# An encoder's expert stage: branches in place on TensorE, full columns in the down matmuls, and three loads moved

## The chip, the cores and the metric
The kernel runs on the 8 cores of one Trainium2 chip. Each core works on one of the 8 sequences of the batch by itself, with no exchange between cores. The metric is the device time of the slowest core in microseconds. Five engines run side by side on each core: TensorE (PE in the profile, its weight loads PEld), VectorE (DVE), ScalarE (ACT), GpSimd (POOL) and SyncE (SP). Here POOL and SP issue nearly all transfers.

## The reference
Input is x (8, 2048, 1024) in float32. Two pre-norm residual layers follow: a token mixer (grouped attention, latent attention and a gated linear attention, merged by gates), then a feed-forward part. In the second layer that part is a mixture of experts, and it is what this case is about:

```
logits = einsum('btd,de->bte', h, w_router)
top_v, top_i = top_k(logits, 2);  top_w = softmax(top_v)
gate = sum over k of top_w * one_hot(top_i, 8)
for e in range(8):
    out += gate[..., e:e+1] * ((silu(h @ w_gate[e]) * (h @ w_up[e])) @ w_down[e])
```

Here h is the RMS-normed x (width 1024) and an expert is 3584 wide. Each token goes to 2 of 8 experts, so of the 2048 tokens of a core 512 go to an expert on average. A last RMSNorm with the gains g_final closes the model.

## The kernel before, in words
**A list of operations.** The program is written as a list: `S.op(engine, fn, reads, writes, ...)` records one operation, a Python function that emits its instructions (one, or many matmuls), with the keys that it reads and writes. `order()` then works out each engine's order from estimated costs, and `run()` emits each engine's stream, with semaphore waits that `waits_for` puts ahead of an operation (L382).

**The expert stage** (`moe`). The router writes for each token the slots that it takes in its two experts (indirect scatters from POOL into a table `mt` in DRAM, L1554). For each expert, `expert_tokens` reads the expert's part of the table (SP, L1576 and L1579), gathers the tokens' rows (five indirect loads from POOL, L1583), and transposes them on TensorE into `xgT` (L1594). `expert_block` then does two stages. In the first, 14 weight blocks `wgu` of 1 MB (three buffers) each give two chunks of 128 hidden columns; `swiglu_chunk` makes for each chunk two TensorE operations (gate, up) of 16 matmuls: 8 steps of the contraction, by two segments of tokens (L1364). ACT and DVE turn them into `aT` (L1374, L1375). In the second, the down stage, 2 halves of the output by 7 weight blocks `wdn` of 0.5 MB (five buffers) give 14 TensorE operations (L1654): `aT` is the stationary side, 128 tokens at a time, and each tile of tokens has a PSUM bank. The results are scaled on ACT and DVE and scattered to DRAM by POOL (L1673). The transposes of the next expert's tokens stand between the first down operations. The last expert also runs the sums (`combine`), and the final norm (`token_rms`, `token_scale`) comes behind it. All weight loads are on POOL's queue; `load_first` issues those of the first expert (3 `wgu`, 5 `wdn`) ahead of the router's end where their buffers are free.

**Levels.** How many tokens an expert gets is known only at run time. `LEVELS = ((512, 256), (560, 256), (608, 304))` gives three sizes with the length of the first segment: at level 0 an operation of the down stage has 4 chunks by 4 tiles of tokens, 16 matmuls; at level 1 there is a fifth tile of 48 tokens, at level 2 of 96, so 20 matmuls. The router leaves each expert's level in `C.level`. TensorE's operations of an expert have the attribute `sel` (expert, address of its level, operation that wrote it) and `alts`, one function for each level. Only TensorE branches. If an expert has more than 608 tokens, all engines enter an overflow section (`cond_section`, L441, L442); it doesn't happen with these inputs.

**Where the branch stands.** `stretches` cuts TensorE's order into groups. An operation without `sel` is a group by itself, but from the first operation of an expert to its last everything is one group, the next expert's transposes with it. `choose` emits a group: it loads the level into a register (L390), and then

```
with eng.If(v > 1):
    body(2)
with eng.Else():
    with eng.If(v > 0):
        body(1)
    with eng.Else():
        body(0)
```

so the code of an expert stands three times in a row, level 2 first. The profile gives the test of the outer `If` to L403, and to L406 both the inner test and the jump over the code of level 0 behind the code of level 1.

Of the kernel before, what the change touches and what calls it, by code (L numbers as in the profile page):

```python
# [6 lines left out]
F32 = mybir.dt.float32  # L7
BF16 = mybir.dt.bfloat16
# [5 lines left out]
D = 1024  # L14
# [4 lines left out]
NEXP = 8  # L19
DFFE = 3584  # L20
# [3 lines left out]
CAP = 608  # L24
CAPT = (CAP + 127) // 128
# [103 lines left out]
class Sched:  # L129
    def __init__(self, nc, es):  # L130
        self.nc = nc
        self.es = es
        self.ops = []
        self.last_writer = {}
        self.readers = {}
        self.dma_sems = {}
        self.dma_last = {}
        self.eng_ops = {e: [] for e in ENGS}
        self.tiles = {}
        self.top = (nc.sbuf_base + 63) // 64 * 64  # L140
        self.uid = 0

    def alloc(self, stack, name, shape, dt):
        off = self.top
# [240 lines left out]
    def choose(self, eng, group, wm):  # L385

        first = self.ops[group[0]]
        level_ap, level_op = first["sel"][1:]
        self.waits_for(eng, {level_op}, wm)
        v = eng.value_load(level_ap)  # L390
        after = {}

        def body(k):
            w = dict(wm)
            for idx in group:
                o = self.ops[idx]
                self.waits_for(eng, o["deps"], w)
                ins = (o["alts"][k] if o["alts"] else o["fn"])(eng)
                if o["needed"]:
                    key, sem, val = self.event(o)  # L400
                    ins.then_inc(sem, 1)
            after.update(w)
# [7 lines that stand above are left out]
        wm.update(after)  # L410

    def stretches(self, ename):

        order = self.eng_ops[ename]
        last = {}
        for n, idx in enumerate(order):
            if self.ops[idx]["sel"] is not None:
                last[self.ops[idx]["sel"][0]] = n
        n = 0
        assert sorted(last.values()) == [last[k] for k in sorted(last)]  # L420
        while n < len(order):
            sel = self.ops[order[n]]["sel"]
            if sel is None:
                yield [order[n]]
                n += 1
            else:
                yield order[n:last[sel[0]] + 1]
                n = last[sel[0]] + 1

    def run(self, ename, eng, final_waits=()):  # L430
        wm = {}
# [1174 lines left out]
def load_gu(C, S, n, s):  # L1606
    S.op("pool", lambda e: e.dma_start(out=C.wgu[s][:], in_=C.dr["wE"][n]), writes=[("wgu", s)], dma=f"wgu{s}")

def load_dn(C, S, n, s):
    S.op("pool", lambda e: e.dma_start(out=C.wdn[s][:], in_=C.dr["wEd"][n // 14, n // 7 % 2, n % 7]), writes=[("wdn", s)], dma=f"wdn{s}")  # L1610

def load_first(C, S):
    for n in range(3):
        load_gu(C, S, n, n)
    for n in range(5):
        load_dn(C, S, n, n)

def expert_block(C, S, ex, m, n, segs, hook=lambda name, i: None, sel=None):
    dr, TT = C.dr, C.TT
    NC = DFFE // 128  # L1620
# [3 lines left out]
    for g in range(NC // 2):  # L1624
        n_ = C.wi
        C.wi += 1
        s = n_ % 3
        if n_ >= C.ahead[0]:
            load_gu(C, S, ex * 14 + g, s)
        wv = C.wgu[s][:].rearrange("p (v c k m) -> p v c k m", v=2, c=2, k=8)  # L1630
        for c in range(2):
# [3 lines left out]
                         lambda a, b, ch=ch: C.aT[:, ch, a:b], [("aT", ch, i) for i in range(len(segs))], sel)  # L1635
        hook("p1", g)
    C.S = saved
    for half in range(2):
        bk = [(half * 5 + i) % 8 for i in range(nt)]
        for q in range(NC // 4):  # L1640
            n_ = C.wj
            C.wj += 1
            s = n_ % 5
            if n_ >= C.ahead[1]:
                load_dn(C, S, ex * 14 + half * 7 + q, s)
            wv = C.wdn[s][:].rearrange("p (c m) -> p c m", c=4)

            def fn(e, q=q, wv=wv, bk=bk, n=n, h=n):
                ins = None
                for c in range(4):  # L1650
                    for i in range((n + 127) // 128):
                        w = min(128, n - i * 128)
                        at = i * 128 if i * 128 < h else HALF + i * 128 - h
                        ins = e.matmul(C.ps[bk[i]][0:w, :], C.aT[:, 4 * q + c, at:at + w], wv[:, c, :], start=(q == 0 and c == 0), stop=(q == NC // 4 - 1 and c == 3))  # L1654
                return ins
            alts = [lambda e, fn=fn, m=m_, h=h if m_ < CAP else m_: fn(e, n=m, h=h) for m_, h in LEVELS] if sel else None
            down = S.op("pe", fn, reads=[("wdn", s)] + [("aT", 4 * q + c, i) for c in range(4) for i in range(len(segs))], writes=[("ps", b) for b in bk], alts=alts, sel=sel)
            hook("p2", half * 7 + q)
            if sel:
                C.behind = [down]  # L1660
        for i in range(nt):
            y_i = C.yi % 4
            C.yi += 1
            yst = C.yst[y_i]
            w = wd[i]
            col = i if w == 128 else CAPT - 1
            sc, rd = C.mtab[m][0:w, col, 2:3].bitcast(F32), [("ps", bk[i]), ("mtab" if w == 128 else "mtabr", m)]
            if i % 2:
                S.op("act", lambda e, yst=yst, b=bk[i], sc=sc, w=w: e.activation(out=yst[0:w, :], in_=C.ps[b][0:w, :], func=AF.Copy, scale=sc), reads=rd, writes=[("yst", y_i)])  # L1669
            else:  # L1670
                S.op("dve", lambda e, yst=yst, b=bk[i], sc=sc, w=w: e.tensor_scalar(out=yst[0:w, :], in0=C.ps[b][0:w, :], scalar1=sc, scalar2=None, op0=ALU.mult),  # L1671
                     reads=rd, writes=[("yst", y_i)])
            S.op("pool", lambda e, yst=yst, col=col, half=half, w=w: e.indirect_dma_start(  # L1673
                out=dr[f"yt{half}"], out_offset=bass.IndirectOffsetOnAxis(ap=C.mtab[m][0:w, col, 1:2], axis=0), in_=yst[0:w, :], in_offset=None),
                reads=[("yst", y_i), ("mtab" if w == 128 else "mtabr", m)], writes=[("yt", ex, i, half)], dma=f"yst{y_i}")

def moe(C):
    S, dr, sbt, TT = C.S, C.dr, C.sbt, C.TT
    ph = C.es.enter_context(ExitStack())
    one = S.arena(C.hbase + NT * D * 4)  # L1680
# [1 line left out]
    C.wgu = [one("wgu", [128, 4096], BF16) for _ in range(2)]  # L1682
    ntail = [(one.at[0] - base[0]) // 2048]
    assert one.at[0] == C.wbase - 8 * T * 2
    C.aT = one("aT", [128, DFFE // 128, CAP], BF16)
    base.append(one.at[0])
    C.xgT = one("xgT", [128, 8, CAPT * 128], BF16)
    C.sgf = [one("sgf", [128, 512], F32) for _ in range(2)]
# [9 lines left out]
    C.wdn += [one("wdn", [128, 2048], BF16) for _ in range(2)]  # L1698
    C.sq = [one("sq", [128, D], BF16) for _ in range(2)]
    ygt = [one("ygt", [128, 512], F32) for _ in range(4)]  # L1700
    C.load_gain(one, 4)
    C.wgu.append(S.arena(S.nc.sbuf_top - 8192)("wgu", [128, 4096], BF16))
    assert one.at[0] <= S.nc.sbuf_top - 8192
    C.wi = C.wj = C.yi = C.ffi = C.wm = 0
# [19 lines left out]
            tail.extend(over("ytl", [128, 512], F32) for _ in range(n))  # L1724
        gi[0] = 0

    load_first(C, S)
    sub = overflow(C)
    S.cond_section(C.flag[0:1, 0:1], "flag", sub)
    ts, m = expert_tokens(C, S, 0, 0, CAP, "tr", [0, 1, 2, 3])  # L1730
    for t in ts:
        t()
    segs = [(0, CAP // 2), (CAP // 2, CAP)]
    for ex in range(NEXP):
        nxt, nm = [], [0]

        def hook(name, i, ex=ex, nxt=nxt, nm=nm):
# [2 lines left out]
                nxt.extend(ts)  # L1740
            if name == "p2" and i < 5 and nxt:
                nxt.pop(0)()
            if ex == NEXP - 1 and name == "p1" and i >= 2:
                for half in range(2):
                    combine(i - 2, 0, half, ygt, "ygt")
# [53 lines left out]
```

How the kernel before makes its waits and increments, by code:

```python
    def waits_for(self, eng, dset, wm):  # L370
        need = {}
        for d in dset:
            key, sem, val = self.event(self.ops[d])
            if val > need.get(key, (None, 0))[1]:
                need[key] = (sem, val)
        for key, (sem, val) in need.items():
            if key[0] == "e":
                if any(k[0] == "e" and k[1] == key[1] and k[2] > key[2] for k in wm):
                    continue
            if wm.get(key, 0) >= val:
                continue
            eng.wait_ge(sem, val)
            wm[key] = val
# [9 lines left out]
        def body(k):  # L393
            w = dict(wm)
            for idx in group:
                o = self.ops[idx]
                self.waits_for(eng, o["deps"], w)
                ins = (o["alts"][k] if o["alts"] else o["fn"])(eng)
                if o["needed"]:
                    key, sem, val = self.event(o)
                    ins.then_inc(sem, 1)
            after.update(w)
# [27 lines left out]
    def run(self, ename, eng, final_waits=()):  # L430
# [16 lines left out]
            else:  # L447
                ins = o["fn"](eng)
            if o["dma"] is not None:
                ins.then_inc(self.dsem[o["dma"]], 16)
            elif o["needed"]:
                key, sem, val = self.event(o)
                ins.then_inc(sem, 1)
        self.wm = wm
        for (e2, name) in final_waits:
            if e2 == ename and name in self.dsem:
                eng.wait_ge(self.dsem[name], self.dma_sems[name]["total"])
```

## Time and profile before

| | |
|---|---|
| runs (3) | 4669.5 us median, 4656.28 to 5200.78 |
| the profiled execution | 4663.14 us |
| its span on the slowest core (3) | 4661.6 us |
| spans of the 8 cores | 4575.8 to 4661.6 us |
| granted TensorE clock | 0.965 to 0.970 of full speed |
| PE, DVE, ACT, POOL busy on core 3 | 90%, 41%, 42%, 19% |
| first expert's first matmul, last expert's last matmul | 3130.8 us, 4613.8 us |

A busy share is an average over stages, and the matmuls' ends are modelled, so what a change is worth is read from the chain of work that ended last and from the stretch that it touches. In that chain a line is a start, a length and what ran in it; "issue" is time in which the engine waited for nothing that the profile shows, and here it holds the branches. All times are from the start of the span.

### The profile page before, as it was taken

To read this page: it belongs to the slowest core of one execution; us is meant where nothing else is said; L and a number is where in the kernel's file an instruction comes from. 1 tells how busy PE (TensorE), PEld (TensorE's weight loads), DVE (VectorE), ACT (ScalarE), POOL (GpSimd) and SP (SyncE) were. 2 spreads that over 40 slices of the span, in tenths; PEclk is the share of its full clock that TensorE was granted. 3 is DMA by queue.
4 is the path that set the end of the run, shared out by engine and by line. 5 is a ranking of instruction groups with operands and counts; after the bars stand their busy time and mean duration, and the time that the engine had idled before them with its cause. 6 is when DMAs were issued, how large, how long until landed. Compare 5 with 4: busy or idle time off the path is not lost.

```text
span 4661.6 us, 73833 instructions; the slowest of 8 cores (4575.8 to 4661.6 us)
## 1 busy us (share of the span) xinstructions
PE 4180.5 (90%) x25337; PEld 2225.0 (48%) x25337; DVE 1926.7 (41%) x3537; ACT 1964.7 (42%) x2884; POOL 907.3 (19%) x959
## 2 busy tenths in 40 slices
PE   5888988899999999898988899959989999998895
PEld 3444433334444444444433344537638647465571
DVE  3767676752331223758585832442102112111133
ACT  5777687852331213777687742321101111011112
POOL 0111222233200000111222233331111211201101
PEclk9999999999999999999999999979999999999998
DMA  4000211032484331000301132538868977677876
GB/s 115 10 11 1 47 33 38 29 63 41 100 188 83 89 78 46 2 10 2 65 29 38 30 62 38 121 61 152 154 121 143 165 126 141 124 133 132 166 160 207
DMA packets 115186, 390.90 MB, mean 84 GB/s; under 512 B 19040, under 2 KB 30688, under 8 KB 95584
## 3 DMA queue, kind: packets, MB, share of 16 engines
q0 software_dynamic: 63856, 275.09, 33.9%
q1 hardware_dynamic: 50928, 110.52, 7.4%
q8 instruction: 245, 4.01, 0.4%
q14 instruction: 157, 1.29, 0.1%
HBM read 576.85 MB, written 49.61 MB: 134 GB/s over the span
## 4 chain that ended last, share of the span: by engine, by line
PE 74%; DVE 7%; issue 7%; DMA 5%; ACT 5%; POOL 1%; DVEq 0%; ACTq 0%; SPq 0%; POOLq 0%
PE ps L1364 22%; PE ps L712 20%; PE ps L1654 10%; PE ps L826 4%; PE ps L834 4%; PE ps L1423 3%; PE ps L835 3%; ACT PTb L831 2%; PE ps L827 2%; ACT PT L831 2%; DMA wgu<-wE 1%; PE ps L1117 1%; DMA ygt<-yt 1%; PE ps L1142 1%; DMA xr<-x 1%
## 5 line engine op out<-in xcount | busy, mean ns | idle before, releaser
L1364 PE MATMUL ps<-xgT,wgu 128*128 128x256 bf16 (+1 forms) x7168 | 854.4, 283 | 102.7 <-issue 78.0
L1364 PEld LDWEIGHTS ps<-xgT,wgu 128*128 128x128 bf16 x7168 | 710.7, 99 | 246.9 <-issue 109.1
L1374 ACT ACTIVATE sgf<-ps 128x304 f32<-128x304 f32 (+1 forms) x536 | 216.6, 451 | 1019.4 <-PE ps L1364 998.1
L1375 DVE TENSOR_TENSOR aT<-ps,sgf 128x304 bf16<-128x304 f32 (+1 forms) x536 | 248.5, 505 | 931.6 <-PE ps L1364 914.0
L831 ACT ACTIVATE PTb<-ps 128x1024 bf16<-128x1024 f32 x512 | 501.7, 1027 | 91.9 <-PE ps L827 78.4
L831 ACT ACTIVATE PT<-ps 128x1024 bf16<-128x1024 f32 x512 | 502.6, 1033 | 73.5 <-PE ps L827 55.3
L1654 PE MATMUL ps<-wdn,aT 128*128 128x512 bf16 (+1 forms) x2072 | 510.9, 383 | 11.9 <-DVE yst L1671 8.9
L712 PE MATMUL ps<-hT,wm 128*128 128x512 bf16 x1536 | 362.5, 380 | 0.0
L1654 PEld LDWEIGHTS ps<-wdn,aT 128*128 128x128 bf16 (+1 forms) x2072 | 179.6, 98 | 337.0 <-issue 194.1
L1364 PE MATMUL ps<-hT,wf 128*128 128x512 bf16 x1408 | 307.0, 381 | 6.7 <-DMA wf<-wF 5.4
L1302 ACT ACTIVATE sg<-ps,vec 128x512 bf16<-128x512 f32 x192 | 131.9, 689 | 345.3 <-PE ps L712 343.7
L712 PEld LDWEIGHTS ps<-hT,wm 128*128 128x128 bf16 x1536 | 150.5, 98 | 181.7 <-issue 2.2
L826 PE MATMUL ps<-qb,kh 128*128 128x512 bf16 x512 | 194.1, 379 | 39.6 <-ACT PTb L831 35.9
L834 PE MATMUL ps<-PT,Va 128*128 128x512 bf16 x512 | 199.3, 389 | 26.0 <-DVE num L850 13.5
L1364 PEld LDWEIGHTS ps<-hT,wf 128*128 128x128 bf16 x1408 | 137.9, 98 | 173.9 <-issue 10.4
L1669 ACT ACTIVATE yst<-ps,mtab 128x512 f32<-128x512 f32 x32 | 20.3, 686 | 475.5 <-PE ps L1654 475.5
L1220 DVE SCALAR_TENSOR_TENSOR Sbf<-Sst,dec,ps 128x128 bf16<-128x128 f32 x512 | 175.6, 343 | 91.2 <-PE ps L1204 36.9
L834 PE MATMUL ps<-PTb,Vb 128*128 128x512 bf16 x512 | 193.7, 378 | 7.3 <-DVE numb L850 4.3
L1671 DVE TENSOR_SCALAR yst<-ps,mtab 128x512 f32<-128x512 f32 (+1 forms) x48 | 34.4, 745 | 399.4 <-PE ps L1654 334.7
L835 PE MATMUL ps<-PT,Va 128*128 128x512 bf16 x512 | 197.3, 385 | 0.0
L827 PE MATMUL ps<-qb,kh 128*128 128x512 bf16 x512 | 194.4, 380 | 0.0
L835 PE MATMUL ps<-PTb,Vb 128*128 128x512 bf16 x512 | 193.8, 379 | 0.0
(239 smaller groups left out, 6241.6 us busy)
## 6 DMA issues: line engine op xcount, KB each, us to landing
wgu<-wE POOLq DMA_DIRECT2D x112, 1024.0 KB, 9.7
wdn<-wEd POOLq DMA_DIRECT2D x112, 512.0 KB, 6.9
xr<-x SPq DMA_DIRECT2D x51, 512.0 KB, 5.1
wf<-wF POOLq DMA_DIRECT2D x22, 1024.0 KB, 10.1
ropeA<-ropeA SPq DMA_DIRECT2D x40, 512.0 KB, 4.0
wm<-wM POOLq DMA_DIRECT2D x48, 384.0 KB, 4.5
x<-xr SPq DMA_DIRECT2D x32, 512.0 KB, 3.9
wCh<-wC POOLq DMA_DIRECT2D x8, 1024.0 KB, 8.4
```

The source lines that it names most:

```text
L712: ins = e.matmul(out, l_, r_, start=(i == 0), stop=(i == n - 1))
L826: e.matmul(ps[b][:], k_ap(2 * kp), q_ap(0), start=True, stop=True)
L827: return e.matmul(ps[b + 1][:], k_ap(2 * kp + 1), q_ap(1), start=True, stop=True)
L831: S.op("act", lambda e, b=b, p_i=p_i: e.activation(out=PT[p_i][:], in_=C.psall[:, b * 512:b * 512 + 1024], func=AF.Exp, scale=scale), read ...
L834: e.matmul(acc[:], v_ap(2 * kp), PT[p_i][:, 0:512], start=(kp == 0), stop=False)
L835: return e.matmul(acc[:], v_ap(2 * kp + 1), PT[p_i][:, 512:1024], start=False, stop=(kp == NT // 2 - 1))
L1220: S.op("dve", lambda e, ch=ch, cur=cur, nb_=nb_, dcol=dcol: e.scalar_tensor_tensor(out=Sbf[nb_][:], in0=Sst[cur][:], scalar=dec[:, dcol:dc ...
L1364: ins = e.matmul(pk[v * n + i][0][:, 0:b - a], w(v, c, k), rhs(k, a, b), start=(k == 0), stop=(k == 7))
L1374: S.op("act", lambda e, pg=pg, sg=sg, m=b - a: e.activation(out=sg[:, 0:m], in_=pg[0][:, 0:m], func=AF.Silu), reads=[pg[1]], writes=[("sgf ...
L1375: S.op("dve", lambda e, pu=pu, sg=sg, m=b - a, a=a, b=b: e.tensor_tensor(out=out(a, b), in0=pu[0][:, 0:m], in1=sg[:, 0:m], op=ALU.mult), r ...
L1423: ins = e.matmul(C.ps[b0 + half], aT[:, c, TT(tl)], wd[:, c, half * 512:(half + 1) * 512], start=(c == 0), stop=(c == NC - 1))
L1654: ins = e.matmul(C.ps[bk[i]][0:w, :], C.aT[:, 4 * q + c, at:at + w], wv[:, c, :], start=(q == 0 and c == 0), stop=(q == NC // 4 - 1 and c ...
```

## The change
Four things change. (1) TensorE's operations of an expert are cut into groups of at most four consecutive ones, and every group has its own three bodies and its own tests; the level is loaded into a register once for each expert. (2) The down matmuls always load 128 columns of `aT`: `aT` gets 128 more columns, set to zero once, and is read as one flat tensor, so that a tile of 48 or 96 tokens takes in columns of the next chunk; the operation then also depends on that chunk. (3) The final gains are loaded when the sixth expert's first block is done, no longer at the start of the expert stage. (4) The loads of the fourth and fifth down weight block of the first expert wait until its last gather has landed.

```
     def choose(self, eng, group, wm):
         first = self.ops[group[0]]
-        level_ap, level_op = first["sel"][1:]
-        self.waits_for(eng, {level_op}, wm)
-        v = eng.value_load(level_ap)
+        ex, level_ap, level_op = first["sel"]
+        if ex not in self.levels:
+            self.waits_for(eng, {level_op}, wm)
+            self.levels[ex] = eng.value_load(level_ap)
+        v = self.levels[ex]
...
     def stretches(self, ename):
-        order = self.eng_ops[ename]
-        last = {}
-        for n, idx in enumerate(order):
-            if self.ops[idx]["sel"] is not None:
-                last[self.ops[idx]["sel"][0]] = n
-        n = 0
-        assert sorted(last.values()) == [last[k] for k in sorted(last)]
-        while n < len(order):
-            sel = self.ops[order[n]]["sel"]
+        group = []
+        for idx in self.eng_ops[ename]:
+            sel = self.ops[idx]["sel"]
+            if group and (sel is None or len(group) == 4 or sel[0] != self.ops[group[0]]["sel"][0]):
+                yield group
+                group = []
             if sel is None:
-                yield [order[n]]
-                n += 1
+                yield [idx]
             else:
-                yield order[n:last[sel[0]] + 1]
-                n = last[sel[0]] + 1
+                group.append(idx)
+        if group:
+            yield group
...
-def load_dn(C, S, n, s):
+def load_dn(C, S, n, s, extra=()):
...
-def load_first(C, S):
+def load_first(C, S, late=None):
     for n in range(3):
         load_gu(C, S, n, n)
     for n in range(5):
-        load_dn(C, S, n, n)
+        if n < 3 or late is None:
+            load_dn(C, S, n, n)
...  expert_block, down stage
-                        w = min(128, n - i * 128)
                         at = i * 128 if i * 128 < h else HALF + i * 128 - h
-                        ins = e.matmul(C.ps[bk[i]][0:w, :], C.aT[:, 4 * q + c, at:at + w], wv[:, c, :], start=..., stop=...)
+                        at += (4 * q + c) * CAP
+                        ins = e.matmul(C.ps[bk[i]][:], C.aTf[:, at:at + 128], wv[:, c, :], start=..., stop=...)
...
-            down = S.op("pe", fn, reads=[("wdn", s)] + [...], ...)
+            down = S.op("pe", fn, reads=[("wdn", s), ("aT", 4 * q + 4, 0), ("aT", 4 * q + 4, 1)] + [...], ...)
...  moe
-    C.aT = one("aT", [128, DFFE // 128, CAP], BF16)
+    width = DFFE // 128 * CAP
+    C.aTf = one("aT", [128, width + 128], BF16)
+    C.aT = C.aTf[:, 0:width].rearrange("p (c t) -> p c t", c=DFFE // 128)
+    S.op("pool", lambda e: e.memset(C.aTf[:, width:width + 128], 0.0), writes=[("aT", DFFE // 128, 0)])
...
-    C.load_gain(one, 4)
+    C.gain = one("gain", [128, D], F32)
...
-    load_first(C, S)
+    load_first(C, S, True)
...
     ts, m = expert_tokens(C, S, 0, 0, CAP, "tr", [0, 1, 2, 3])
+    for n in (3, 4):
+        load_dn(C, S, n, n, [S.last_writer[("xs", CAPT - 1)]])
...  in hook
+            if ex == NEXP - 3 and name == "p1" and i == 0:
+                S.op("sp", lambda e: e.dma_start(out=C.gain[:], in_=dr["gains"][4]), writes=["gain"], dma="gain", extra=[S.last_writer[("aT", 0, 0)]])
```

## Rows read from the trace of the kernel before
**Rows 1.** The cores: span and mean granted TensorE clock.
```profile
core 3: 4661.6 us, clock 0.969
core 4: 4638.5 us, clock 0.968
...
core 7: 4589.6 us, clock 0.965
```
**Rows 2.** Chain that ended last, core 3, expert stage: start us, us, what.
```profile
3090.06 13.33 DMA mt<-meta,idx
...
3121.60 9.17 issue
3130.77 100.18 PE ps L1364 x896
...
3258.65 24.35 PE ps L1654 x112
...
3284.59 2.48 issue
...
3441.28 36.36 PE ps L1654 x140
...
3479.22 15.35 issue
...
3843.16 11.08 issue
```
**Rows 3.** The same view of core 1, a down stage at level 2.
```profile
3793.28 30.39 PE ps L1654 x140
```
**Rows 4.** Branch lines, core 3: all of L403, all of L406, then L406 in two windows.
```profile
L403 PEldq COMPARE_BRANCH  x8: 4737/7302/8697, 3120.5 to 4403.4; - x8
...
L406 PEldq COMPARE_BRANCH  x13: 70/4795/6972, 3125.3 to 4610.2; - x13
...
L406 PEldq COMPARE_BRANCH  x1: 6878/6878/6878, 3473.7 to 3473.7; - x1
...
L406 PEldq COMPARE_BRANCH  x1: 3457/3457/3457, 4610.2 to 4610.2; - x1
```
**Rows 5.** Down line L1654, core 3, 3441 to 3478 us: ns min/median/max, first and last start.
```profile
L1654 PE MATMUL ps<-wdn,aT x140: 376/379/397, 3441.3 to 3477.2; 128*128 128x512 bf16 x112, 128*48 128x512 bf16 x28
```
**Rows 6.** Groups of instructions: the 48-column down matmuls of cores 3, 4 and 7.
```profile
L1654 PE MATMUL ps<-wdn,aT 128*48 128x512 bf16 x280 | 111.2, 397 | 0.0
L1654 PE MATMUL ps<-wdn,aT 128*48 128x512 bf16 x168 | 66.7, 397 | 0.0
L1654 PE MATMUL ps<-wdn,aT 128*48 128x512 bf16 x56 | 22.2, 397 | 0.0
```
**Rows 7.** DMA queues, PE's code (packets, MB): 3131 to 3231, 3479 to 3495 us.
```profile
q8 instruction: 7, 0.11, 0.5%
...
q8 instruction: 5, 0.08, 3.1%
```
**Rows 8.** Stretches: us, then PE, PEld, DVE, ACT, POOL busy (count), PEclk, DMA share, GB/s.
```profile
3131.00:3231.00 100.00, 100.00 (x900) 88.85 (x899) 23.21 (x54) 20.75 (x56) 6.96 (x13) 0.98 0.76 136
...
3495.00:3505.00 10.00, 9.92 (x66) 7.54 (x65) 1.51 (x3) 0.91 (x3) 0.00 (x0) 0.72 0.00 0
3600.00:3654.00 54.00, 51.09 (x267) 24.02 (x265) 6.08 (x10) 4.56 (x6) 13.02 (x20) 1.00 0.93 163
```
**Rows 9.** Timeline of PE, fifth weight block of the second and third expert.
```profile
3323.55 6.69 PE L1364 MATMUL ps<-xgT,wgu 128*128 128x256 bf16 x43 [3.16 <-DMA wgu<-wE]
...
3528.49 1.86 PE L1364 MATMUL ps<-xgT,wgu 128*128 128x256 bf16 x8 [2.65 <-DMA wgu<-wE]
```
**Rows 10.** Timeline of SP at the head of the expert stage.
```profile
3087.90 0.33 SPq L727 DMA_DIRECT2D gain<-gains  x1
3107.85 0.37 SPq L1576 DMA_DIRECT2D mtab<-mt  x1
```
**Rows 11.** DMA issues of the whole kernel: count, KB, median us to landing.
```profile
mt<-meta,idx POOLq DMA_INDIRECT x32, 4.9
```

More of the change, by code:

```diff
@@ L141, in __init__ @@
         self.uid = 0
+        self.levels = {}
     def alloc(self, stack, name, shape, dt):
@@ L1607, in load_gu @@
     S.op("pool", lambda e: e.dma_start(out=C.wgu[s][:], in_=C.dr["wE"][n]), writes=[("wgu", s)], dma=f"wgu{s}")
-def load_dn(C, S, n, s):
-    S.op("pool", lambda e: e.dma_start(out=C.wdn[s][:], in_=C.dr["wEd"][n // 14, n // 7 % 2, n % 7]), writes=[("wdn", s)], dma=f"wdn{s}")
-def load_first(C, S):
+def load_dn(C, S, n, s, extra=()):
+    S.op("pool", lambda e: e.dma_start(out=C.wdn[s][:], in_=C.dr["wEd"][n // 14, n // 7 % 2, n % 7]), writes=[("wdn", s)], dma=f"wdn{s}", extra=extra)
+def load_first(C, S, late=None):
     for n in range(3):
@@ L1651, in fn @@
                     for i in range((n + 127) // 128):
-                        w = min(128, n - i * 128)
                         at = i * 128 if i * 128 < h else HALF + i * 128 - h
-                        ins = e.matmul(C.ps[bk[i]][0:w, :], C.aT[:, 4 * q + c, at:at + w], wv[:, c, :], start=(q == 0 and c == 0), stop=(q == NC // 4 - 1 and c == 3))
+                        at += (4 * q + c) * CAP
+                        ins = e.matmul(C.ps[bk[i]][:], C.aTf[:, at:at + 128], wv[:, c, :], start=(q == 0 and c == 0), stop=(q == NC // 4 - 1 and c == 3))
                 return ins
             alts = [lambda e, fn=fn, m=m_, h=h if m_ < CAP else m_: fn(e, n=m, h=h) for m_, h in LEVELS] if sel else None
-            down = S.op("pe", fn, reads=[("wdn", s)] + [("aT", 4 * q + c, i) for c in range(4) for i in range(len(segs))], writes=[("ps", b) for b in bk], alts=alts, sel=sel)
+            down = S.op("pe", fn, reads=[("wdn", s), ("aT", 4 * q + 4, 0), ("aT", 4 * q + 4, 1)] + [("aT", 4 * q + c, i) for c in range(4) for i in range(len(segs))], writes=[("ps", b) for b in bk], alts=alts, sel=sel)
             hook("p2", half * 7 + q)
```

## The prediction
> **What bounds the kernel now.** Read first the cores: the time is that of the slowest, core 3, 4661.6 us in the profiled execution, and core 4 stands only 23 us below it [rows 1]. TensorE sets the pace from the router on, so the chain that ended last on core 3 is the view to read next [rows 2]: eight experts, each 896 gate and up matmuls and then fourteen down operations, with a stretch called "issue" (no wait that the profile shows) ahead of each. These gaps have three sizes. With 512 tokens or fewer (level 0, 16 down matmuls an operation) TensorE's sequencer takes two branches to reach the body; with more (level 1) one, and another at its end, past the body of level 0. The gap is 2.48 us where one branch is taken, 9.17 and 11.08 where two are, 15.35 where three are; core 3 has three, three and two gaps of these kinds. The branches themselves are in the trace [rows 4]: 4.7 to 8.7 us at L403, 6.9 us for the one that starts at 3473.7, 3.46 us for the last one, when the DMA queues are nearly empty; 0.07 us (the least at L406) is one not taken. The second thing to see is the down stage. 140 matmuls, of which 28 load 48 columns, take 36.36 us on core 3 [rows 2, 5]; 140, of which 28 load 96 columns take 30.39 us on core 1 [rows 3]. The narrow weight load can't hide behind the matmul before it. Nothing ahead of the router's end is touched.
>
> **Full down columns.** Each 48-column matmul falls from (36.36 - 112 x 24.35/112) / 28 = 0.43 us to 0.217 [rows 2]. That is 5.97 us for each half of an expert, 11.9 for an expert. Core 3 has 280 such matmuls, 56 for an expert, so five experts: 59.7 us; core 4 has three, 35.8 us; core 7 one, 11.9 [rows 6]. This lies on TensorE, which the chain never leaves there, so all of it counts. The added columns give rows of PSUM that nobody reads. The extra dependencies (the next chunk of aT, and a small memset on POOL) are long met when the down stage begins: nothing. If the next chunk weren't ready, the first down operation would wait for one DVE product; no more.
> The Trainium skill, "TensorE: Matmul & The Clock Gate", section on fast weight load, says that this mode is on only with 128 weights. By that the 96-column loads of level 2 would gain too, 11.9 us more for each such expert. The trace disagrees: at 30.39 us for 140 they already run at 0.217 us.
>
> **Branches in place.** Removed are the far branches: 3 x 2.48 + 3 x 10.1 + 2 x 15.35 = 68 us of gaps [rows 2]. After such a gap TensorE also runs a while at the lower of its two clocks: 66 matmuls in 9.92 us, where 900 take 100 us, so 2.6 us a gap, 18 us in all [rows 8]. Together 86. Not all is won. Behind the down stage POOL still issues the scatters of the results, the gathers for the next expert and the fourth and fifth weight loads, in that order. The fifth lands 39.0 us after the down stage ended at 3284.59 with a short gap, and 49.3 us after 3479.22 with the long one [rows 2, 9]. TensorE without a gap would want it after 256 matmuls, 28.4 us. So up to 10 us a transition comes back as a wait for weights, or nothing where they land in time: 0 to 70 us for seven. I take 5 each, 35, because four of the seven transitions of this core show such a wait (two of them are in the rows). Net gain 51 us.
>
> Added are 19 groups an expert (56 gate and up operations by four make 14; the transposes of the next expert's tokens cut the 14 down operations into 1, 1, 4, 4, 4), 152 in all, each with two taken branches or one taken ahead and one behind. These targets are near, and the trace of before has no near branch. What it has is the fetching of code: 7 fetches for 900 matmuls with their 900 weight loads [rows 7], so one page is about 256 instructions, 16 KB, every 14 us; and 5 fetches between 3479 and 3495 us, where two branches are taken, so a taken far branch brings its target and the page behind it, and by that one page is kept ahead. A body of four gate and up operations is 64 matmuls, with waits a little over half a page; three bodies are 1.6 pages, in 7.0 us. So a page is entered every 4.4 us instead of 14, and the jump of a group lands on the page ahead, which was asked for when the last one was entered. In half of the groups that happened inside the body, at a moment even over 7 us. If a fetch takes L, such a group waits L x L / 14 us on average when the sequencer has no lead, and (L - lead)^2 / 14 with its full lead. The lead is the time from 3473.7, when the branch is reached, to 3477.2, when the last matmul before it starts [rows 4, 5]: 3.5 us, some 14 matmuls of 0.26, hence about 1.7 us of gate and up matmuls at 0.11. L is between 3.46 us and 6.9 [rows 4]. I take 4.7, the shortest at L403, because that branch had gathers in flight, and the gate and up stretch has a DMA share of 0.76 against 0.93 in a down stage [rows 8]. For 56 such groups: 4 x 4.7^2 = 88 without lead, 4 x 3.0^2 = 36 with it; 60 taken. For the 40 down groups, of which some 22 cross a page in the body, L is 6.9, the lead 3.5, the body about 15 us: 8 to 35; 12 taken. A wait of over 2 us brings the lower clock again; ten of them at 2 us: 20. Sum 92, bounds 0 (all pages there in time) and 280 (L 6.9 everywhere, no lead, 60 us of lower clock). While TensorE waits for code the weights catch up, so 20 of the 35 above are counted twice.
>
> **Head of the experts.** At 3087.9 SP issues the load of the final gains, and a down weight follows on POOL. Both lie in the rings ahead of the last routing scatter, which lands in 13.33 us against a median of 4.9 [rows 2, 10, 11]; SP can read the slot table only at 3107.85. With the gains gone to the sixth expert and two down weights behind the gathers, the scatter should land in its median: 8.4 us, of which I take 8 (0 if SP's own far branch past the overflow code is what is late, 13 if that speeds up too). The load of two down weights behind the landed gathers blocks POOL until the gathers are in; queued behind are weight loads that wait for TensorE anyway, and these weights are needed 100 us later [rows 2]: nothing. The gains at the sixth expert put 512 KB among the weights: 0 to 8 us, covered by the transition's term. SP waits for aT there, with only the next slot tables behind it: nothing.
>
> **The sum**, for core 3: 4661.6 - 59.7 - 51 - 8 = 4542.9, + 92 - 20 = 4614.9. Core 4: 4638.5 - 35.8 - 59 + 72 = 4615.7. Core 7: 4589.6 - 11.9 - 59 + 72 = 4590.7. So two cores tie for the slowest near 4616. The profiled execution took 4663.1 with its 1.5 us outside the span, and the median of the runs is 4669.5; half of that distance added gives **4620**.
>
> **Rivals.**
> 1. *The pages are there in time.* The branch term is near zero and the time 4545 to 4575. For: L of 3.46 us with the full lead gives 12 us. Against: most far branches took well over 5 us with weights in flight [rows 4]. Chance 0.28, and the case for over 2% faster (below 4576).
> 2. *Code fetch becomes the bound.* With twice to three times the pages, each at 6.9 us, the gate and up groups wait 190 us, the down groups 34, and the clock adds 60: 4543 + 284 - 20 = 4807. It decides from L of about 6.2 us, where the term passes 240 us and the time 4763. For: half of the branches at L403 took 7.3 us or more [rows 4]. Against: these came in transitions, with scatters, gathers and weights in the rings together. Chance 0.15, slower.
> 3. *Every taken branch fetches its target*, even one that is held. Two a group at 4.7, less 1.7 of lead: 7.7 x 152 = 1170 us, some 5700 us. The trace has no near branch that excludes it. Chance 0.07, slower. The Trainium skill, "Runtime: NRT & Kernel Launch", section "Instruction fetch mechanics", says that only a taken branch whose target isn't in the two-page window forces a fetch, which speaks against this rival; no row here shows it.
> 4. *The weights are the bound*, and what TensorE gains comes back as waits for wgu. A down stage at a share of 0.93 [rows 8] speaks for it, 0.76 in the gate and up stretch against. If all the gaps come back and the columns half, 4661.6 - 30 - 8 = 4624 for core 3, so about 4630. Chance 0.07.
>
> **How the numbers follow.** The forecast has 0.43. Within 2% (about what a measurement of this kernel can tell from no change) are the forecast and rival 4: 0.50; faster 0.28; slower 0.22. The range leaves out rival 3, most of rival 2 and the ends of rival 1: 4535 to 4770.
>
> **What would show it.** Down stages of level 1 at 30.4 us for 140 matmuls. No gap over 5 us ahead of an expert. About 28 code fetches an expert instead of 10. "Issue" idle ahead of L1364 spread in waits of 1 to 4 us at group starts; if there are none, rival 1; if every group has one of 7, rival 3. The last routing scatter landing in about 5 us. The forecast is wrong if the near branches' wait per group averages below 0.2 us or over 1.5.

## The result, and the profile after

The changed kernel is **2.5% slower**: its time stands to that of the kernel before as 1.0249 [1.0186 to 1.0311], with single runs of 4778.6 and 4779.2 us against 4656.3 to 4669.5 us. 4620 us was forecast, 4535 to 4770 the range: the time lies above it. The first profile of the changed kernel fell into an execution with one die at a lower clock, so the rows below are from a second profile of the same kernel, in which all eight cores have the same clock (4793.3 us; the kernel before took 4688.9 and 4693.9 us on that chip, a ratio of 1.022).

The cores (answers to [rows 1]):
```profile
core 3: 4791.1 us, clock 0.964
core 4: 4791.7 us, clock 0.959
...
core 7: 4750.9 us, clock 0.962
```
Before, core 7 was 72 us ahead of core 3; now it is 40 us ahead. Core 3 lost 129.5 us and core 7 161.3: whatever was added is paid by every core, and core 7, which wins only one expert's narrow columns, pays it almost bare. The two profiles are from two chips. On the chip of the second one core 3 took 4687.3 and 4692.3 us with the kernel before, so 26 to 31 of its 129.5 us are not the change's.

Core 3 can be compared piece by piece. The chain that ended last, where the third expert's gate and up stage begins (answers to [rows 2]):
```profile
3496.42 30.39 PE ps L1655 x140
...
3537.86 11.98 PE ps L1364 x82
3549.84 3.20 issue
3553.04 6.85 PE ps L1364 x46
3559.89 0.42 issue
3560.31 7.15 PE ps L1364 x64
3567.45 3.39 issue
3570.85 15.81 PE ps L1364 x128
3586.66 2.59 issue
3589.25 10.75 PE ps L1364 x97
```
The down half of a level 1 expert takes 30.39 us, as forecast, and the long "issue" ahead of an expert is gone. But the stage that was one row of 896 matmuls in 100.18 us is now cut up: 64 or 128 matmuls (one or two groups), then in most places 2.6 to 3.4 us of "issue", over and over. The waits of this stage, for the first expert (engine, line, waited for, total us, times, longest):
```profile
PE ps L1364 <- issue: 26.5, 10, 4.2
```
One of the ten, of 3.6 us, stands ahead of the stage's first matmul, nine are inside. The same stage as a stretch (answers to [rows 8], the columns are those):
```profile
3133.40:3265.60 132.20, 109.28 (x896) 92.10 (x897) 23.21 (x54) 20.69 (x56) 6.93 (x13) 0.91 0.64 114
```
And the code fetched in it (answers to [rows 7]):
```profile
q8 instruction: 22, 0.36, 1.0%
```
The same 896 matmuls take 132.2 us in place of 100; TensorE stands idle for 23 of them, and its granted clock is 0.91, not 0.98: a larger part of the stretch at 1.2 GHz in place of 2.4 GHz, behind the waits. The DMA share has fallen from 0.76 to 0.64, and no matmul of this stage waits for weights. 22 pages of code came in where 7 did. The groups of the whole kernel on core 3 (busy us, mean ns, idle us before them):
```profile
L1364 PE MATMUL ps<-xgT,wgu 128*128 128x256 bf16 (+1 forms) x7168 | 906.6, 291 | 200.3 <-issue 173.8
```
In the kernel before, this group was busy for 854.4 us.

The branches themselves (answers to [rows 4]):
```profile
L392 PEldq TENSOR_LOAD <-level x8: 303/308/324, 3129.0 to 4513.2; - x8
L406 PEldq COMPARE_BRANCH  x151: 207/337/8045, 3129.4 to 4730.2; - x151
L409 PEldq COMPARE_BRANCH  x245: 70/187/7452, 3130.0 to 4738.5; - x123
```
L406 is now the test at the head of a group (L403 before), L409 the inner test and the jumps over the bodies that are left out (L406 before). Half of the 151 tests are over in 0.34 us and half of the 245 others in 0.19, taken or not; the longest take 8.0 and 7.5 us. In the eight gate and up stages of core 3, 222 of the 280 branches take under 1.5 us, and 58 take 1.5 to 6.7.

That the long ones wait for their page can be seen from the packets of the code queue. At one of them, one row for the branch, then the code queue's line for 3149.5 to 3149.7 us and for 3155.8 to 3155.9 us (there is no packet of it between 3147.7 and 3149.5 nor between 3149.7 and 3155.8):
```profile
L409 PEldq COMPARE_BRANCH  x1: 4232/4232/4232, 3147.8 to 3147.8; - x1
...
q8 instruction: 1, 0.02, 28.5%
...
q8 instruction: 1, 0.02, 57.5%
```
The branch is reached at 3147.8; the page's packet starts at 3149.6 and takes 0.9 us, the branch ends at 3152.0, 1.5 us after it, and the packet of the next page starts 3.8 us later. So it is at all 58: each ends 1.3 to 1.6 us after a packet has landed, and the next packet starts 3.7 us after the branch's end in the median (the middle half 2.3 to 4.4). With 0.9 us for the packet these three pieces make 6.1 us from one page's entry to the next.

Measured from matmul to matmul, core 3 of the two profiles adds up as follows (sums over the eight experts):

| stretch of core 3 | before | after | difference |
|---|---|---|---|
| first expert's first matmul at | 3130.8 | 3133.4 | +2.6 |
| gate and up stages | 879.2 | 1100.7 | +221.5 |
| down stages | 533.1 | 503.5 | -29.6 |
| gaps between experts | 70.9 | 4.3 | -66.6 |
| behind the last down matmul | 47.8 | 49.0 | +1.2 |
| span | 4661.6 | 4791.1 | +129.5 |

The differences add up to +129.1. In which stretch the 26 to 31 us between the chips lie isn't shown; they are small against the +221.5. The columns and the gaps brought what they should; one term, the gate and up stages, swallowed all of it and more.

### The profile page after: what moved, and what is told of

Read it like the earlier page. It is cut to its first block, busy times and chain, and to the rows that moved or that the text cites. A ratio compares the mean times of both kernels' runs of the same rounds, so it can differ in the third digit from the quotient of the medians.

```text
span 4860.2 us, 73945 instructions; the slowest of 8 cores (4749.7 to 4860.2 us)
## 1 busy us (share of the span) xinstructions
PE 4262.4 (88%) x25225; PEld 2298.7 (47%) x25225; DVE 1929.3 (40%) x3537; ACT 1970.9 (41%) x2884; POOL 905.7 (19%) x960
## 4 chain that ended last, share of the span: by engine, by line
PE 76%; issue 9%; DVE 6%; DMA 5%; ACT 4%; POOL 1%; SPq 0%; DVEq 0%; ACTq 0%; another core or an unknown queue 0%; POOLq 0%
PE ps L1364 23%; PE ps L712 20%; PE ps L1655 8%; PE ps L826 4%; PE ps L834 4%; PE ps L835 4%; PE ps L1423 3%; PE ps L827 2%; ACT PT L831 1%; ACT PTb L831 1%; PE ps L1117 1%; DMA yt<-yst,mtab 1%; PE ps L1142 1%; DMA xr<-x 1%; DMA wf<-wF 1%
## 5 line engine op out<-in xcount | busy, mean ns | idle before, releaser
L1364 PE MATMUL ps<-xgT,wgu 128*128 128x256 bf16 (+1 forms) x7168 | 896.6, 290 | 221.2 <-issue 187.1
L1364 PEld LDWEIGHTS ps<-xgT,wgu 128*128 128x128 bf16 x7168 | 729.8, 103 | 388.4 <-issue 244.1
L1655 PE MATMUL ps<-wdn,aT 128*128 128x512 bf16 x1960 | 436.8, 384 | 34.1 <-issue 21.4
L1655 PEld LDWEIGHTS ps<-wdn,aT 128*128 128x128 bf16 x1960 | 191.2, 99 | 271.2 <-issue 53.0
L826 PE MATMUL ps<-qb,kh 128*128 128x512 bf16 x512 | 209.1, 408 | 29.0 <-ACT PTb L831 25.3
L834 PE MATMUL ps<-PT,Va 128*128 128x512 bf16 x512 | 208.2, 407 | 22.0 <-DVE num L850 12.1
L1607 POOL DMA_DIRECT2D wgu<-wE x112 | 60.7, 542 | 880.9 <-PE ps L1364 816.7
L834 PE MATMUL ps<-PTb,Vb 128*128 128x512 bf16 x512 | 208.5, 407 | 6.5 <-DVE numb L850 4.4
L827 PE MATMUL ps<-qb,kh 128*128 128x512 bf16 x512 | 210.5, 411 | 0.0
L835 PE MATMUL ps<-PTb,Vb 128*128 128x512 bf16 x512 | 208.8, 408 | 0.0
L835 PE MATMUL ps<-PT,Va 128*128 128x512 bf16 x512 | 206.9, 404 | 0.0
L712 PE MATMUL ps<-hT,wCh 128*128 128x512 bf16 x768 | 197.4, 405 | 3.5 <-DVE eg L1256 1.8
```

The costliest lines, as they stand in the source:

```text
L712: ins = e.matmul(out, l_, r_, start=(i == 0), stop=(i == n - 1))
L826: e.matmul(ps[b][:], k_ap(2 * kp), q_ap(0), start=True, stop=True)
L827: return e.matmul(ps[b + 1][:], k_ap(2 * kp + 1), q_ap(1), start=True, stop=True)
L834: e.matmul(acc[:], v_ap(2 * kp), PT[p_i][:, 0:512], start=(kp == 0), stop=False)
L835: return e.matmul(acc[:], v_ap(2 * kp + 1), PT[p_i][:, 512:1024], start=False, stop=(kp == NT // 2 - 1))
L1364: ins = e.matmul(pk[v * n + i][0][:, 0:b - a], w(v, c, k), rhs(k, a, b), start=(k == 0), stop=(k == 7))
```

## The experiments

### The parts, each alone
Four kernels. The first is the changed kernel with the branches as before (columns and moved loads stay), the others are one part alone.

```diff
# e1_far: choose() and stretches() as before: one group for an expert
# e2_cols: e1_far, and the loads where they were
-    C.gain = one("gain", [128, D], F32)
+    C.load_gain(one, 4)
-    load_first(C, S, True)
+    load_first(C, S)
# e3_inplace: the kernel before with the new choose() and stretches()
# e4_loads: e1_far, and the narrow down columns of before
-                        ins = e.matmul(C.ps[bk[i]][:], C.aTf[:, at:at + 128], ...)
+                        ins = e.matmul(C.ps[bk[i]][0:w, :], C.aT[:, 4 * q + c, at:at + w], ...)
```

> Full columns and the moved loads, with the branches left as before (one group for each expert). Theory: what makes the changed kernel slow is the fetching of code by the near branches alone, since three bodies for every four operations pass 1.6 pages of code in 7 us and a page takes 5 to 7 us to come while weights are in flight. So this one keeps the gaps of before (68 us on core 3) and gains 60 us on core 3 by the columns and about 8 at the head: about 4600 us in a fast run, ratio 0.985 to 0.99, gate and up stages of 100 to 110 us as before. Rival A: the columns or the moved loads cost the time (a later gain load among the weights, an extra dependency): then it is above 4663 and the gate and up stages are long here too. Rival B: weights are the bound and the saved time comes back: 4640 to 4660.

> Full columns alone. Theory: 11.9 us for each expert of level 1, so core 3 from 4662 to about 4602 and core 4 from 4638 to about 4603; ratio about 0.988. 140 down matmuls of level 1 in 30.4 us. Rival B (weights are the bound): the gap or the waits ahead of L1364 grow by what the down stage loses, ratio 0.995 to 1.

> Branches in place alone, with narrow columns and the loads as before. Theory: the gate and up stages grow by 25 to 35 us each as in the changed kernel, and the down stages of level 1 are 76 us again: 4790 to 4840 us, ratio 1.03 to 1.035. Rival A: near 4663 or below, since the gaps are gone and the guilty parts are left out.

> The moved loads alone (gains at the sixth expert, two down weights behind the gathers). Theory: the last routing scatter lands in about 5 us instead of 13 and the first expert starts 8 us earlier on core 3; nothing is lost at the sixth expert: 4655 us, ratio 0.998. Rival: 512 KB of gains among the weights delay the sixth expert by up to 8 us: ratio 1.000.

| kernel | ratio to the kernel before |
|---|---|
| columns and loads | 0.988 [0.979 to 0.998] |
| columns alone | 0.986 [0.978 to 0.994] |
| branches in place alone | 1.037 [1.029 to 1.045] |
| loads alone | 0.997 [0.992 to 1.001] |
| all (the change) | 1.025 [1.019 to 1.031] |

The parts multiply: 0.988 x 1.037 = 1.025. Columns are the whole gain, branches in place the whole loss, and the loads are nothing that can be measured. The branches alone, at 4845.0 to 4854.8 us, came out a little above what was expected (4790 to 4840). On core 3 the gate and up stages, from first to last matmul, sum to 879 us before, 876, 873 and 893 in the three kernels with far branches, and 1091 with branches in place alone, so the loss sits in these stages in every profile taken. In the chain of core 3 with columns and loads, the gap is still there and the half of the down stage is short:
```profile
3420.35 30.39 PE ps L1656 x140
3452.32 11.98 issue
```
The eight down stages of that core sum to 473.8 us against 533.1: 59.3 us less, where 59.7 was forecast. That is a ratio of 0.987 by itself; with its earlier start and shorter gaps core 3 came down by 84 us, to 4577.8, but it is then no longer the slowest (the spans are 4557.7 to 4589.4 us), so the time follows it only in part.

The loads alone start core 3's experts at 3128.2, against 3130.8, where 8 us were expected. Over the eight cores the mean start is 3136.3 before, 3135.5 with the loads alone, 3140.8 with the columns alone, 3129.6 in the changed kernel; single cores move by 10 us either way. So the head gives 1 to 7 us, if the moved loads are what gives it: with two levels in place (below), where the head is the same code, the mean start is 3120.6.

The branches alone show the loss with nothing else in play. The stretch of the second expert's gate and up stage on core 3, columns as in [rows 8]; 114.2 us before:
```profile
3314.90:3454.70 139.80, 117.48 (x897) 91.46 (x896) 25.27 (x57) 22.22 (x58) 17.32 (x24) 0.93 0.67 123
```

### Is it the branch or the page that is paid for?
Shorter groups double the branches and leave the code that is passed the same. Leaving the weight loads out leaves both and empties the DMA rings.

```diff
# e7_n2
-            if group and (sel is None or len(group) == 4 or ...
+            if group and (sel is None or len(group) == 2 or ...
# e8_noweights: from the second expert on, no load of wgu and wdn (they compute with what lies in the buffers)
-        if n_ >= C.ahead[0]:
+        if n_ >= C.ahead[0] and (ex == 0 or S is not C.main):
```

> As the changed kernel, with groups of at most two operations: twice as many groups and branches, the same code in all. Theory (pages are what is paid for): the same 1.6 pages in 7 us, gate and up stages of 128 to 135 us, 4775 to 4800 us. Rival C (a price for each taken branch): the excess of 30 us a stage doubles, 5000 us or more.

> The changed kernel without the weight loads of experts two to eight, which compute with the first expert's weights (a part of the computation is left out). Theory: the code waits because the DMA rings are full of weights; with them empty a page takes 3.5 us and 4.4 us pass between pages, so from the second expert on the gate and up stages of level 0 fall from 130 to about 100 to 105 us, those of level 1 to 110. Rival E (the time of a page is the sequencer's own, whatever else is in the rings): stages of 125 us or more.

With groups of two the ratio is 1.012 [1.008 to 1.015], 4732.8 us: faster than with groups of four. The gate and up stages of core 3 are near those with groups of four (131.9, 141.8, 131.4, 127.3, 132.6, 126.5, 131.3, 153.3 us; 1076 in all, with four 1101), so twice the branches cost nothing, and the pages are still paid for. But 4775 to 4800 us was expected, and the kernel is faster than that: core 3 is 59 us shorter than with groups of four (on another chip), 25 in the gate and up stages, 23 in the down stages, where five of the eight have no wait for code left, 9 in an earlier start of the first expert and 3 ahead of the seventh. Why was not settled; shorter jumps are a possible reason. The second expert's stage as a stretch, then its code:
```profile
3308.60:3450.40 141.80, 118.24 (x898) 91.11 (x897) 25.27 (x57) 22.17 (x58) 17.24 (x24) 0.92 0.69 126
```
```profile
q8 instruction: 23, 0.38, 1.1%
```
Without weights it took 4566.3 us in a single run. The first expert still has its weights and takes 123.9 us for the gate and up stage with 20 us of waits; the second to seventh take 103 to 113, with 3 to 7 us of waits. The second expert's, as a stretch, then its code:
```profile
3317.50:3428.30 110.80, 107.43 (x897) 87.42 (x896) 25.27 (x57) 22.17 (x58) 9.64 (x10) 1.00 0.09 26
```
```profile
q8 instruction: 21, 0.34, 1.3%
```
21 pages in 110.8 us: a page every 5.3 us, with hardly a wait, and the clock stays at 1.00. So 5.3 us is the pace of the stage here; a fetch takes less. The 20 branches over 1.5 us that are left in the second to eighth expert's stages end 1.4 to 1.5 us after a packet of 1.0 us has landed, as with weights, but the next packet starts 0.8 us after the branch's end in place of 3.7: about 3.2 us from entry to entry. With the weights in the rings it is a page every 6.0 us (22 in 132.2) or 6.2 (23 in 141.8), and TensorE waits for them. So code fetch is slow because its packets start late while weights are in the rings, and the stage takes as long as its pages take.

### Fewer pages: two levels
If pages are the bound, two bodies in place of three take it away: the one for up to 560 tokens is left out, and such an expert does the work of 608 tokens (segments of 304 and 304).

```diff
-LEVELS = ((512, 256), (560, 256), (CAP, HALF))
+LEVELS = ((512, 256), (CAP, HALF))
-        with eng.If(v > 1):
-            body(2)
+        with eng.If(v > 0):
+            body(1)
         with eng.Else():
-            with eng.If(v > 0):
-                body(1)
-            with eng.Else():
-                body(0)
+            body(0)
# e5_two_far: on e1_far    e6_two_inplace: on the changed kernel
# e9_two_n2: e6_two_inplace with groups of two
```

> As e1 (full columns, moved loads, one group for each expert), but with two levels, 512 and 608 tokens, so one test and two bodies. An expert with over 512 tokens computes 304 + 304 columns in the first stage instead of 256 + 304: 4.5 us more. Each expert has one taken far branch less ahead of a level 0 body, and one less ahead of one above 512 it doesn't have: gaps of 2.5 us behind an expert of level 0 and about 9 behind the others. Both theories of the near branches say the same: 8 branches fewer of about 5.5 us against 5 x 4.5 us, so some 20 us under e1, about 4570, ratio 0.982.

> As the changed kernel, but with two levels, so two bodies for each group of four. Theory (one page of code ahead, and a page takes 5.5 to 7 us to come): a gate and up group passes 271 instructions, 1.06 pages, in 7 us, so the code just keeps up: gate and up stages of level 0 at 102 to 112 us instead of 130, no gaps, 4590 to 4630 us. Rival C (each taken branch has a cost of its own of 1.5 to 2 us): the level 0 groups lose one of two taken branches, so the excess falls only by half, to 115 us a stage, about 4690. Rival D (a taken branch drops what was fetched ahead): as C or worse.

> The changed kernel with two levels (512 and 608 tokens, one test a group), and groups of at most two operations in place of four. Theory (code fetch is paid by the page entered, and two bodies make about one page for each 17 us of gate and up work where three make 1.6): the same pages pass for the same work, whatever the length of a group. So the gate and up stages stay at 103 to 106 us for an expert of up to 512 tokens and 117 to 121 us above, the down stages at 52 and 64 us, and the ratio to the kernel before at 0.98, within 0.01 of the kernel with two levels and groups of four. Rival (each taken branch has a price of its own, which shows once the pages are no longer the bound): 100 more groups with one taken branch each, at 0.3 us some 30 us more, ratio 0.988.

**Two levels in place beat the kernel before and the changed one**: 0.981 [0.977 to 0.985], 4589.7 us. Over the columns and loads with far branches (0.988 [0.979 to 0.998]) no gain is shown, as the two intervals overlap. The gate and up stage of core 3's second expert as a stretch, then its code, then a line of its timeline:
```profile
3282.50:3402.60 120.10, 117.60 (x898) 88.33 (x897) 25.26 (x57) 22.17 (x58) 17.26 (x24) 0.99 0.79 145
```
```profile
q8 instruction: 14, 0.23, 0.7%
```
```profile
3293.46 109.30 PE L1361 MATMUL ps<-xgT,wgu 128*128 128x304 bf16 x832 [2.50 <-DVE yst L1669]
```
832 matmuls in one row, through some 13 groups and their branches, with no wait between them. 14 pages in 120 us are one every 8.6 us; in the 103 us of the first expert (up to 512 tokens) they are one every 7.4 us, and that stage too is near its 100 us. The price is the wider segment: 117 to 121 us where level 1 takes 109 with three levels. That is 8 to 12 us an expert, more than I had allowed.

Two levels with far branches gave no interval; its runs of 4594.1 and 4600.5 us (4570 was expected) stand at 0.983 to 4678.4 us, the median of seven of the kernel before. So with one far branch an expert in place of two or three, most of the gaps are gone too (0.2, 10.0, 0.2, 1.2, 0.9, 7.2, 0.2 us on core 3), and a gain of the near branches over that (0.981 to 0.983) isn't shown. Groups of two: 4578.6, 4583.3 and 4587.8 us, against 4688.9 and 4693.9, or 0.977, again without an interval. The 136 more groups cost nothing that can be seen (the gate and up stages of core 3 sum to 932 us, with groups of four 930; the down stages to 466 in both):
```profile
3288.60:3408.30 119.70, 117.53 (x897) 88.29 (x896) 25.26 (x57) 22.14 (x58) 17.25 (x24) 0.99 0.77 145
```
The rival (0.3 us for each taken branch, 0.988) is out.

### Level 2 far, levels 0 and 1 in place
Shortened; `parts()` cuts an expert's operations into groups of four.
```diff
+        with eng.If(v > 1):
+            body(2, group, dict(wm))          # once for the whole expert
         with eng.Else():
+            for part in parts():               # groups of four
+                with eng.If(v > 0): body(1, part, dict(w))
+                with eng.Else():    body(0, part, wa)
```

> The changed kernel, but the body of level 2 stands once for a whole expert ahead of the others, reached and left by far branches as in the kernel before, and only levels 0 and 1 stand in place, two bodies in groups of four. Theory: an expert of level 1 has its segments of 256 and 304 tokens back, which is some 8 us less gate and up work than 304 and 304; an expert of level 0 or 1 enters its section by one taken far branch over the body of level 2, 5 to 7 us of fetch less 3.5 us of lead, and some 2.6 us of lower clock behind it. So the gate and up stage of level 1 at 109 to 115 us, gaps of 2 to 6 us ahead of an expert, time within 10 us of the kernel with two levels in place, ratio 0.98. If the fetch at the entry costs its full 7 us as ahead of the experts in the kernel before, it is 20 us slower than that, ratio 0.985; if two bodies in a row with shorter code for level 1 wait less, 20 us faster, ratio 0.976.

It took 4633.1 us against 4688.9 and 4693.9, 0.988 from a single time: faster than before, outside what was expected (0.976 to 0.985), and no better than two levels. The reason is partly elsewhere: cores 2 and 3, the slowest, start their experts at 3169.5 and 3168.4 us, over 30 us behind the other six (3120.5 to 3136.0). SP, which also reads the slot table, is held there by issuing one group of transfers (timeline of SP):
```profile
3086.35 27.87 SPq L1476 DMA_DIRECT2D h<-hbr  x4
3142.39 0.37 SPq L1596 DMA_DIRECT2D mtab<-mt  x1
```
The changed kernel shows 12.7 us at the same place on core 3, the kernel before 0.3. Why it is so long here was not tried. In the expert stage itself the mechanism is as expected: core 3's fifth and sixth expert, both of level 1, pass 848 matmuls through the in-place branches without a wait, 107.0 and 107.7 us for the stage, and the gaps ahead of the experts are 2.7 to 8.3 us.
```profile
3870.42 101.21 PE ps L1384 x848
```
From the first expert to the last down matmul core 3 needs 1407.7 us here and 1405 with two levels in place: the two prices, wider segments and a far branch, cancel.

### The changed kernel again


> The changed kernel again, for a profile beside the others. Theory: 4780 us, gate and up stages of 127 to 153 us on every core, in which TensorE stands idle for 21 to 29 us in eight to ten waits and runs the rest at a lower granted clock; cores within 30 us of one another.

4793.3 us; gate and up stages of core 3 of 128.6 to 157.2 us, with 21 to 40 us of waits in 9 to 11 places; cores within 41 us of one another, where 30 were expected. The stages are as expected but for the last expert's, which takes 144 to 162 us over the eight cores and is the longest in the kernel before as well (128.9 us on core 3).

## Why the prediction was wrong

**The failing step** is the price of the near branches: "If a fetch takes L, such a group waits L x L / 14 us ... I take 4.7 ... Sum 92". On core 3 the gate and up stages grew by 221.5 us, and the down stages are 29.7 us over the 473.8 of the kernel with columns and loads: 251 in all against 92, the lower clock counted in both (up to 31 of the 251 may be the chip's). Two things were wrong in it.

1. *The model.* It took each group's fetch as independent, with a wait only where the page had been entered lately; at 4.7 us such waits are short. But one page is fetched at a time, and the next isn't asked for until that one is entered. The prediction itself worked out that a page is entered every 4.4 us. With a fetch longer than that, the fetches form a chain of their own and the stage lasts pages times fetch, whatever the place of the jump. 22 pages at 6.0 us are 132 us; less 100 for an expert of level 0, 32, less 109 for level 1, 23; three and five of them on core 3 give 211, where 221.5 were measured. The 6.0 us is the first expert's own 132 us divided by its 22 pages, so for that stage the sum shows nothing; the 6.1 us added up from packets and branches is what backs it, and the second to seventh expert have 20 to 22 pages at 6.1 to 6.7 us. Comparing 4.4 us with the L of 4.7 to 6.9 in the same part would have shown the danger. The runs with fewer pages, with more branches and without weights bear this out. No row shows a request; that the next page is asked for only at the entry of the one before it is read from its packet, which starts 0.65 us or more after every branch that had to wait.
2. *The size of L.* 4.7 us was taken as the gate and up stage has less traffic than a transition. It is 6.0 there. The one error needs the other: at 4.7 us the chain gives 22 x 4.7 = 103 us and would hardly have lengthened a stage of 100, and at 6.0 the prediction's own formula gives 74 to 144 us of waits for the gate and up groups, where the profile has 174 of "issue" ahead of them. The "against" of rival 2 was the same argument and fell with it.

Rival 2 happened: code fetch is the bound, and its 4807 us stand against 4779 to 4793. Its price was worked out by the same formula with L at 6.9, so that it came so near is partly luck. Its chance of 0.15 was too low: half of the branches at L403 had taken 7.3 us or more [rows 4], and the forecast used their minimum.

**The other steps**, with what was measured on core 3:
- *Full columns*: forecast 59.7 us, measured 59.3 (columns and loads). A half of 140 matmuls without a wait in it now takes the 30.39 us that those with 96-column loads took before. Right.
- *Far branches gone*: gaps of 68 us forecast, 9.2 of them ahead of the first expert. From matmul to matmul the gaps between experts lost 66.6 us, and the "issue" ahead of the first fell from 9.17 to 2.95. Right, and a little under. The lower clock behind them (18 us) can't be told apart, as the new waits bring more of it.
- *Weights that come back as waits* (35, less 20): not seen in the changed kernel, where the code leaves the weights time (DMA share 0.64). With two levels in place, where TensorE isn't held up, the second to seventh expert of core 3 have 1.3 to 5.6 us of waits each, a size like that of the term, but by luck: of 21 us in these six stages the profile puts 2.1 to weights and 16.7 to something that the prediction hadn't named. Behind the first weight block TensorE needs a PSUM bank of the down stage before it, whose copy to `yst` waits until an earlier scatter of `yst` has landed (chain of core 3, third expert):
```profile
3468.94 8.38 DMA yt<-yst,mtab
...
3477.41 0.76 DVE yst L1669
...
3478.30 15.81 PE ps L1361 x128
```
- *Near branches in the down stages*: 12 forecast, 29.7 measured; same error.
- *Head*: 8 forecast; -2.6 on core 3, 7 in the mean of the cores. On core 3 the last routing scatter lands in 4.13 us, as forecast, but is issued at 3108.5 in place of 3090.1, and the gathers land in 7.15 in place of 4.85. Why the router's end is later was not tried.
- *Lower clock behind the new waits*: 20 forecast. The group of gate and up matmuls is busy for 52 us more than before (906.6 less 854.4), with part of the 18 us behind the old gaps taken off.
- *What would show it*: 28 code fetches an expert were forecast in place of 10. Over the eight experts of core 3 they went from 107 to 231, so from 13.4 to 28.9 for each: right. Waits in the middle of the stage, of 1 to 4 us: their size is right (2.6 us in the mean, 4.2 the longest), but there are 9 or 10 for the 14 groups of a stage. The bound given for a wrong forecast, over 1.5 us a group in the mean, was too loose: 1.3 us of waits in 152 groups were enough once the lower clock came on top.

**Rivals 1, 3 and 4** are out. Rival 1 (pages there in time) would be true with two levels. Rival 3 (each taken branch fetches its target) is excluded by the median of 0.34 us at L406 and of 0.19 at L409. The Trainium skill, "Runtime: NRT & Kernel Launch", section "Instruction fetch mechanics", says that a taken branch forces a fetch when its target is outside the two-page window. The trace agrees as far as most near branches have none: 222 of 280 take under 1.5 us. The same section says that crossing a page is mostly hidden, since instructions issue more slowly than pages arrive. The trace agrees for straight code (7 pages in 100 us, no waits) and disagrees where most of a page is jumped over. Rival 4 (weights are the bound) is excluded by the fall of the DMA share.

## What to carry to other kernels
A branch costs little; what costs is the code that it jumps over. Count the pages that a stage passes, dead bodies included, and divide the stage's time by them: if that is less than one fetch takes under the stage's own DMA traffic (6 us here), the stage lasts as long as its code takes to come in. So put only few and short alternatives in place. Three bodies in place cost 3.7% by themselves (2.5% with the 1.2% of columns and loads taken off); two bodies, even with more arithmetic, won 1.9%, columns and loads included. But two bodies left far, with the same columns and loads, stood at 0.983: two in place are clearly better than three in place, but that it pays to have them in place rather than far is not shown. And where two durations stand side by side in an estimate, the interval between requests and the time that one takes, compare them first: above one, waits no longer average out but add up.

## What was not expected of the hardware
- TensorE's code comes in at 16 KB per 6.0 us, 2.7 GB/s, in a stage in which the core's DMA engines move 114 GB/s. The packet itself takes 0.9 us of it; 3.7 us pass before it starts, and 1.5 from its end to the end of the branch. With a DMA share of 0.09 the 3.7 us are 0.8.
- A near branch that doesn't wait takes 0.2 to 0.34 us, and none of it reaches TensorE's matmuls: with two levels in place 832 matmuls in groups of four ran through in one row, and with groups of two 807.
- The granted clock of the first expert's stage was 0.91 with nine waits inside of 2.5 us in the mean, and 0.98 in the kernel before, without them.
- Once the transition has no gap, the next expert waits 1.1 to 4.1 us for a PSUM bank whose copy waits for a scatter of 8.4 us.
- SP can be held for 27.9 us in issuing transfers of the router's rows, which had taken 0.3 us before, in a kernel whose code for that part is the same. This stays open.
